# Retention's v projected with tokens as rows, in a hybrid decoder layer

## The reference

```python
proj = hn @ w_in
..., rq, rk, rv, rg, gate_a, gate_b = jnp.split(proj, SPLIT_IDX, axis=-1)
rq = rotary(rq.reshape(B, L, RET_HEADS, RET_DK), pos)
rk = rotary(rk.reshape(B, L, RET_HEADS, RET_DK), pos)
o_b = retention_chunked(rq, rk, rv.reshape(B, L, RET_HEADS, RET_DV))
...
inner = einsum('bhncs,bhnse->bhnce', einsum('bhncd,bhnsd->bhncs', q, k) * dmask, v)
def step(S, xs):
    in_c, qd_c, kd_c, v_c = xs
    o_c = in_c + jnp.einsum('bhcd,bhde->bhce', qd_c, S)
    S = S * g_chunk + jnp.einsum('bhcd,bhce->bhde', kd_c, v_c)
    return S, o_c
```

## Time and profile before

| | |
|---|---|
| median of 3 runs | 2141.28 us (2135.45 to 2142.12) |
| the profiled execution: its time | 2140.7 us |
| the profiled execution: its span | 2138.9 us |
| TensorE busy | 2085.0 us (97%) |
| VectorE busy | 1134.9 us (53%) |
| ScalarE busy | 634.3 us (30%) |
| GpSimd busy | 287.6 us (13%) |
| mean granted TensorE clock | 0.991 of full speed |
| line 733, projection matmuls | 5688 in three groups of 1896, 618.2 + 610.6 + 608.5 us busy |
| share of the last chain on TensorE | 85% |

### The profile page before, as it was taken

The page is one execution under the profiler, slowest core; times in us unless marked ns, Lnnn a source line. Parts: engine busy times, 40 slices in busy tenths (PEclk is TensorE's granted clock), DMA queues, the critical chain, the costliest instruction groups (busy, mean ns, idle before and its releaser), DMA issues.

```text
span 2138.9 us, 30674 instructions
## 1 busy us (share of the span) xinstructions
PE 2085.0 (97%) x13250; PEld 2003.1 (94%) x13250; DVE 1134.9 (53%) x1283; ACT 634.3 (30%) x805; POOL 287.6 (13%) x277
## 2 busy tenths in 40 slices
PE   7999999989999999999999999999999999999997
PEld 6999999989999999999999999999999999999995
DVE  4443454766656655556534333365656455565556
ACT  4212323533333443353433332321111111111112
POOL 0000002586360212112100001100000000000002
PEclk9999999989999999999999999999999999999999
DMA  7222225654444554454342321120111111111102
GB/s 207 80 107 93 81 93 175 217 168 111 128 128 128 154 158 136 120 131 125 98 155 91 116 79 50 40 89 30 50 50 59 41 39 50 50 50 32 58 30 79
DMA packets 156764, 207.36 MB, mean 97 GB/s; under 512 B 33230, under 2 KB 118102, under 8 KB 156502
## 3 DMA queue, kind: packets, MB, share of 16 engines
q1 hardware_dynamic: 156630, 205.40, 30.8%
HBM read 151.85 MB, written 53.52 MB: 96 GB/s over the span
## 4 chain that ended last, share of the span: by engine, by line
PE 85%; DVE 5%; POOL 3%; DMA 2%; ACT 2%; issue 2%; SPq 0%; POOLq 0%; DVEq 0%; ACTq 0%
PE a_psum L733 33%; PE a_psum L138 29%; PE a_psum L1012 11%; PE a_psum L801 1%; PE a_psum L718 1%; DVE post L1400 1%; POOL ext L1789 1%; PE a_psum L818 1%; POOL y L1785 1%; PE a_psum L798 1%; PE a_psum L741 1%; PE a_psum L844 1%; PE a_psum L921 1%; DMA w_raw<-in_w_in 1%; PE a_psum L936 1%
## 5 line engine op out<-in xcount | busy, mean ns | idle before, releaser
L733 PE MATMUL a_psum<-xh,w_hi 128*128 128x348 f32 (+1 forms) x1896 | 618.2, 326 | 4.8 <-ACT post L1126 3.7
L733 PE MATMUL a_psum<-xl,w_hi 128*128 128x348 f32 (+1 forms) x1896 | 610.6, 322 | 0.0
L733 PE MATMUL a_psum<-xh,w_lo 128*128 128x348 f32 (+1 forms) x1896 | 608.5, 321 | 0.0
L733 PEld LDWEIGHTS a_psum<-xh,w_hi 128*128 128x128 f32 x1896 | 358.6, 189 | 9.2 <-ACT post L1126 4.6
L733 PEld LDWEIGHTS a_psum<-xl,w_hi 128*128 128x128 f32 x1896 | 358.9, 189 | 0.7
L733 PEld LDWEIGHTS a_psum<-xh,w_lo 128*128 128x128 f32 x1896 | 358.5, 189 | 0.0
L1126 ACT ACTIVATE post<-a_psum 128x348 f32<-128x348 f32 (+1 forms) x234 | 107.2, 459 | 611.6 <-PE a_psum L733 585.6
L1058 ACT ACTIVATE w_hi<-w_raw 128x1024 fp32r<-128x1024 f32 x131 | 138.3, 1055 | 436.8 <-PE a_psum L138 409.3
L138 PE MATMUL a_psum<-xh,w_hi 128*128 128x342 f32 (+1 forms) x1104 | 234.4, 320 | 6.2 <-DVE xl L1352 6.2
L138 PE MATMUL a_psum<-xl,w_hi 128*128 128x342 f32 (+1 forms) x1104 | 234.5, 320 | 0.0
L1333 DVE TENSOR_TENSOR w_lo<-w_raw,w_hi 128x1024 fp32r<-128x1024 f32 x131 | 168.4, 1286 | 123.4 <-ACT w_hi L1058 123.4
(11 more groups left out here) (209 smaller groups left out, 2546.6 us busy)
## 6 DMA issues: line engine op xcount, KB each, us to landing
w_raw<-in_w_in SPq DMA_DIRECT2D x79, 512.0 KB, 3.6
mix_scratch<-post SPq DMA_DIRECT2D x48, 522.0 KB, 3.1
w_raw<-in_w_up SPq DMA_DIRECT2D x44, 512.0 KB, 3.5
ext<-mix_scratch SPq DMA_DIRECT2D x9, 1536.0 KB, 8.5
y<-mix_scratch SPq DMA_DIRECT2D x27, 512.0 KB, 5.6
down_raw<-in_w_ffn_down SPq DMA_DIRECT2D x22, 512.0 KB, 4.5
ext<-grow_scratch SPq DMA_DIRECT2D x9, 512.0 KB, 5.5
ext<-mix_scratch SPq DMA_DIRECT2D x9, 512.0 KB, 6.8
```

What stands on the lines that cost most here:

```text
L733: mm = pe.matmul(psum[:, u % 2, 0:n], w[:, k, :], x[:, k, at0 + n * j:at0 + n * j + n], start=(k == 0 and part == 0), stop=(k == KC - 1 an ...
```

## The change

Tokens become the rows of v's projection: the stationary operand is a block of x (128 channels by the tokens of a chunk, 16 for the first), the moving one is 512 or 256 columns of weights. The 24 units of v are now 9 of one chunk with 512 columns (the first four weight tiles), then 7 and 8 units with 256 columns, of one or two chunks each (`RV_STEPS`). The four tiles of the first part are all split before its first unit, into `va` in the memory of `y`; the next two go to the usual slots and the last two to `vb2` in `y`. `front_plan` gets its own places for these loads and splits. Each unit is stored by itself into a new DRAM scratch `rvt` (chunk, token, channel) from two stage buffers, and `r_load` loads a chunk of it as it is used, in two buffers (`rvs`). `r_trv` and its copy are gone; `r_in` has 16 tiles rather than 24. Since `y` is taken until the first part is done, `inv` waits for it (`RV_B`), its first batch begins behind u = 34 (before: 38), with `tout` 0 and `tin` 1 behind u = 55 and `comp` 8 behind u = 59, and the `mst` steps stand behind u = 28, 29, 31, 32, 34, 37, 40, 43, 46 (before: 29, 31, 34, 36, 39, 41, 44, 46, 49). The core of the diff:

```diff
+RV_STEPS = ([(0, 512, (c,)) for c in range(9)]
+            + [(512, 256, c) for c in ((0,), (1,), (2, 3), (4, 5), (6,), (7,), (8,))]
+            + [(768, 256, c) for c in ((0,), (1,), (2,), (3, 4), (5,), (6,), (7,), (8,))])
+RV_A, RV_B, RV_C = 3 * T_RV, 3 * T_RV + 9, 3 * T_RV + 16
...
+    splits_at = {(T_RV - 2, 1): (T_RV,), (T_RV - 2, 2): (T_RV + 1,), (T_RV - 1, 0): (T_RV + 2,), (T_RV - 1, 1): (T_RV + 3,),
+                 (T_RV, 0): (T_RV + 4,), (T_RV, 2): (T_RV + 5,), (T_RV + 3, 0): (T_RV + 6,), (T_RV + 3, 2): (T_RV + 7,)}
+    loads_at = {(T_RV - 3, 1): (T_RV,), (T_RV - 3, 2): (T_RV + 1,), (T_RV - 2, 1): (T_RV + 2, T_RV + 3),
+                (T_RV - 1, 1): (T_RV + 4,), (T_RV, 0): (T_RV + 5,), (T_RV, 2): (T_RV + 6,), (T_RV + 3, 0): (T_RV + 7,),
+                (T_RV + 3, 2): (T_Q,)}
...
-        at = 29 + 5 * c // 2
+        at = (28, 29, 31, 32, 34, 37, 40, 43, 46)[c]
...
-    u = 38
+    u = 34
     for b in range(NBATCH):
         steps[u].append(("tin", b))
         if b == 1:
-            steps[u].append(("comp", NCH - 1))
+            steps[u + 4].append(("comp", NCH - 1))
...
-        u += 1
+        u += 5 if b == 0 else 1
         steps[u].append(("tout", b))
...
+                    if T_RV <= t < T_Q:
+                        pe.wait_ge(w_lo, T_RV + (4 if u < RV_B else 6 if u < RV_C else 8))
+                        pe.wait_ge(evac, u - 1)
+                        at0, n, chunks = RV_STEPS[u - RV_A]
+                        for i, c in enumerate(chunks):
+                            rows_ = META if c == 0 else CH
+                            x0 = FRONT if c == 0 else FRONT + META + CH * (c - 1)
+                            for k in range(KC):
+                                hi, lo = ((x[:, k, :] for x in va) if u < RV_B else (x[:, :, k, :] for x in vb1)
+                                          if u < RV_C else (x[:, k, :] for x in vb2))
+                                for part, (w, x) in enumerate(((hi, xh), (hi, xl), (lo, xh))):
+                                    mm = pe.matmul(psum[0:rows_, u % 2, n * i:n * i + n], x[:, k, x0:x0 + rows_], w,
+                                                   start=(k == 0 and part == 0), stop=(k == KC - 1 and part == 2))
+                        mm.then_inc(units_done, 1)
+                        continue
...
-                elif kind == "r_trv":
-                    c = a[0]
-                    if c + 1 < NCH:
-                        pe.wait_ge(d_rkd, c + 1)
-                    else:
-                        pe.wait_ge(d_rS, 4 * c)
-                    turn(r_in[:, 16:24, :], 2).then_inc(pe_rtv, 1)
                 elif kind == "r_out":
                     c = a[0]
-                    pe.wait_ge(a_rv, c + 1)
+                    pe.wait_ge(rv_ld[c % 2], 16 * (c // 2 + 1))
...
-                    sp.dma_start(r_in, mix[:, S_RQ:S_RQ + 24, c * CH:c * CH + CH]).then_inc(r_ld, 16)
+                    sp.dma_start(r_in, mix[:, S_RQ:S_RQ + 16, c * CH:c * CH + CH]).then_inc(r_ld, 16)
+                    if c == 0:
+                        for n in range(2):
+                            sp.wait_ge(rv_stored[n], 16 * 12)
+                        sp.wait_ge(units_done, 3 * T_Q)
+                    elif c >= 2:
+                        sp.wait_ge(pe_rst, 4 * (c - 1))
+                        sp.wait_ge(pe_ro, c - 1)
+                    sp.dma_start(rvs[c % 2].rearrange("p h c -> p (h c)"), sc["rvt"][c]).then_inc(rv_ld[c % 2], 16)
...
                     if j0 == 0:
+                        pool.wait_ge(units_done, RV_B)
                         pool.wait_ge(d_tout, 2 * b)
```

More of the change, by code:

```diff
@@ L165, in front_plan @@
     add = plan.append
+    splits_at = {(T_RV - 2, 1): (T_RV,), (T_RV - 2, 2): (T_RV + 1,), (T_RV - 1, 0): (T_RV + 2,), (T_RV - 1, 1): (T_RV + 3,),
[3 more added lines that the diff above has]
+                (T_RV + 3, 2): (T_Q,)}
     def unit(t, j):
-        if j == 0:
+        if j == 0 and not T_RV - 1 <= t < T_Q - 1:
             add(("split", t + 1))
+        for n in splits_at.get((t, j), ()):
+            add(("split", n))
         add(("proj", t, j))
     def weights(t, j):
-        if j == 0:
+        if j == 0 and not T_RV - 2 <= t < T_Q - 1:
             add(("load", t + 2))
+        for n in loads_at.get((t, j), ()):
+            add(("load", n))
     add(("intro",))
@@ L240, in front_plan @@
         weights(t, j)
-        if j == 2:
-            add(("conv", t) if conv_tile(t) else ("rvstore", t))
+        if not conv_tile(t):
+            add(("rvstore", 3 * t + j))
+        elif j == 2:
+            add(("conv", t))
     units = [(t, j) for t in range(T_ZB, T_END) for j in range(3)]
@@ L355, in program @@
         w_raw = sb("w_raw", [P, KC, P])
-        wh = [sb(f"w_hi{s}", [P, KC, P], F32R) for s in range(SLOTS)]
-        wl = [sb(f"w_lo{s}", [P, KC, P], F32R) for s in range(SLOTS)]
+        wh2, wl2 = (sb(n, [P, SLOTS, KC, P], F32R) for n in ("w_hi", "w_lo"))
+        wh, wl = ([x[:, s, :, :] for s in range(SLOTS)] for x in (wh2, wl2))
         post = [sb(f"post{s}", [P, T]) for s in range(5)]
@@ L371, in program @@
         o_hi, o_lo = sb("o_hi", [P, GH, P], F32R), sb("o_lo", [P, GH, P], F32R)
+        row_bytes = 4 * T
+        va = [sb(f"v_w4_{n}", [P, KC, 4 * P], F32R, over=place["y"] + 4 * row_bytes * n) for n in range(2)]
+        vb1 = [wh2, wl2]
+        vb2 = [sb(f"v_w2b_{n}", [P, KC, 2 * P], F32R, over=place["y"] + 2 * row_bytes * n) for n in range(2)]
+        diag = sb("diag", [P, GH, P], over=place["o_hi"])
+        rv_st = sb("rv_stage", [P, 2, 512], over=place["o_lo"])
         free = place["a_cst"] + -(-4 * C_HEAD // 32) * 32
@@ L410, in program @@
         abT = y[0:2 * GH, 0:2, :].rearrange("p k t -> p (k t)")[:, 0:TW]
-        rkd, rv, rqd, r_osq, r_ro, r_ost = (yrow(n) for n in range(6))
-        xtmp, diag = y[:, 6, 0:256], yrow(7)
-        r_in = erow(0, 3072)
+        rkd, rqd, r_osq, r_ro, r_ost = (yrow(n) for n in (0, 2, 3, 4, 5))
+        rvs = (yrow(1), erow(2048))
+        xtmp = y[:, 6, 0:256]
+        r_in = erow(0, 2048)
         rS = ext[:, 3072:5120].rearrange("p (h a e) -> p h a e", h=RH, a=2)
@@ L539, in stored_up_to @@
                 for n in range(2):
-                    sp.wait_ge(stored[n], 16 * (8 + sum(1 for m in range(T_K, t + 1) if m % 2 == n)))
+                    sp.wait_ge(stored[n], 16 * (8 + sum(1 for m in (*range(T_K, T_RV), *range(T_Q, T_ZB))
+                                                        if m <= t and m % 2 == n)))
             for step in plan:
@@ L797, in _ @@
                             o = four(4 + n // 4)[:, n % 4, seen(c)]
-                            mm = pe.matmul(o, rv[:, n, :], rsc[:, h, seen(c)], start=True, stop=(c == 0))
+                            mm = pe.matmul(o, rvs[c % 2][:, n, :], rsc[:, h, seen(c)], start=True, stop=(c == 0))
                             if c:
@@ L1107, in _ @@
                     elif T_RV <= t < T_Q:
[L1108 to L1110 removed]
+                        if u >= RV_A + 2:
+                            act.wait_ge(rv_stored[u % 2], 16 * ((u - RV_A) // 2))
+                        n, rows_ = RV_STEPS[u - RV_A][1] * len(RV_STEPS[u - RV_A][2]), CH
+                        if RV_STEPS[u - RV_A][2] == (0,):
+                            rows_ = META
+                        dst, src = rv_st[0:rows_, u % 2, 0:n], psum[0:rows_, u % 2, 0:n]
                     elif t < T_ZB:
```

75 lines of the change are left out of this document (49 added, 26 removed).

## The result

| | before | after |
|---|---|---|
| median, run beside each other | 2138.84 us (2135.45 to 2142.12) | 2124.51 us of six runs, 2124.18 us of the five that the ratio uses |
| ratio after / before | | 0.9932 (95% interval 0.992 to 0.9944) |
| the profiled execution: its time | 2140.7 us | 2124.18 us |
| its span | 2138.9 us | 2122.4 us |
| mean granted TensorE clock | 0.991 | 0.995 |

The changed kernel takes 0.68% less by the ratio (14.5 us), 14.7 us less by the median of its five runs, and 16.5 us less by the two profiled executions; the forecast had 15.7 us between profiled executions, and 2125.0 us. Five of the six runs of the changed kernel lie between 2121.88 and 2127.12 us; the sixth took 4149 us and has no part in the ratio.

What follows compares the result with a forecast made beforehand. TensorE, busy 97% of the span, and its few waits bound the kernel. +9.4 - 8.3 - 13.0 - 5.8 + 2.0 = -15.7 us against 2140.7 us gave 2125.0 us (chance 0.69), range 2115 to 2141 us.

Steps and rivals of the forecast that it cites:

- Term 1: v's projection as rows: 216 matmuls of 512 columns and 432 of 256 (0.117 us, unmeasured) replace 576: +9.4 us.
- Rival C: Matmuls of 256 columns don't run at the longer ones' rate; at 0.231 us each +49.1 us, 2174 us; chance 0.08.
- Term 2: Nine groups of eight transpositions of v go from TensorE, 0.92 us each: -8.3 us.
- Term 3: TensorE's 8.6 us wait before line 798 (`r_out` 0) and 4.4 us of low clock behind it go: -13.0 us.
- the edit takes this chain apart twice: Before line 798: no copy of v left to wait for, and `comp` 8 moves behind `tin` 1; within the -13.0 us.
- The layout of the inversion: GpSimd's inversion begins at 393.5 us and ends near 458, `tout` 0 is due near 472; no longer last.
- Rival D: The wait moves: the inversion holds `r_out` or the next loads, Term 3 gives half; 2132 us; chance 0.06.
- Term 4: TensorE's waits for `rkd` (line 1441) in two chunks, 4.2 us, and 1.6 us of lower clock go: -5.8 us.
- Term 5: Work moved and added around v's projection and Retention's first state copies: +2 us, between 0 and 12.
- (b, c): In v's stage, short units' evacuations (margins 1.5 and 0.7 us) and SP's 24 stores: 1 us together.
- rival B: Between steps 37 and 47 short units outrun ScalarE, VectorE and stores: 12 us instead of 2, 2135 us; chance 0.17.
- (e): At step 55 `tout` 0 and `tin` 1 stand before Retention's first state copies on VectorE: 1 us.

## Why the prediction was right

**Term 1 (+9.4): right.** v's projection takes 101.1 us for 101 predicted. 512 columns came every 0.232 us (0.2335), 256 every 0.118 (0.117). The unmeasured price was the step by which the forecast could most easily fall, and it lay on the line through the two rows. Rival C is out. The 7.7 to 8.3 us of the meta tokens' leftover products confirm that columns set the cost, however few are stationary.

**Term 2 (-8.3): right.** Eight groups added again cost 7.2 to 8.7 us, 7.4 in the stage; nine at that price are 8.3.

**Term 3 (-13.0): the size was right, the reason half wrong.** The wait and the low clock are both gone (26.64 us busy at 1.00 in the 27 us where it was 18.41 at 0.75). But "the edit takes this chain apart twice" failed: each cut was counted as enough by itself. Moving `comp` 8 alone is enough (13.0 us over the stretch of the wait, 12.7 in the median). Taking away the copy of v alone isn't: with `comp` 8 beside `tin` 1 the changed kernel loses 7.0 us in the stage, since line 1241 is held. The prediction asked who needs the copy of v, not what stands next in ScalarE's order behind the held copies. The layout of the inversion held; GpSimd in the changed kernel:

```profile
397.08 0.95 POOL L1852 MEMSET ext<- 128x1024 f32 x1
...
453.75 1.27 POOL L1864 TENSOR_TENSOR ext<-ext,y 128x31 f32<-128x31 f32 x1
```

It began 3.6 us later than the 393.5 predicted and ended at 455.0, 3 us earlier than 458; `tout` 0 was at 471.2 (472). Rival D is out for the changed kernel; in the kernel with exchanged turns and the old places of the inversion it was there, 4.19 us.

**Term 4 (-5.8): right in kind, the size not shown.** Put back, the wait costs 7.3 us in the stage and 8.9 in the median, but this is the wait of the new plan (5.7 us); in the old plan it was 4.2 us of waiting and 1.6 of clock. The 1.6 was one execution's: with `comp` 8 moved alone, the clock stayed at 1.00 behind the same wait.

**Term 5 (+2): right in size, from one of its parts.** The feeding (b, c) cost 0 and not 1: the stage of v has no wait. The evacuation that step 41 needs was laid out for 411.6, that for step 47 at 435.6; ScalarE's rows:

```profile
408.71 2.71 ACT L1264 ACTIVATE ext<-post 32x256 f32<-32x256 f32 x4 [3.31 <-DVE post L1566]
...
411.45 0.87 ACT L1206 ACTIVATE rv_stage<-a_psum 128x256 f32<-128x256 f32 x2
...
431.04 2.76 ACT L1264 ACTIVATE ext<-post 32x256 f32<-32x256 f32 x4 [2.22 <-DVE post L1566]
...
434.78 0.64 ACT L1206 ACTIVATE rv_stage<-a_psum 128x256 f32<-128x256 f32 x2
```

Each row of line 1206 holds two evacuations, and the unit needs the first of the two. That one ended at 411.83, 0.34 us ahead of the start of the unit's first matmul at 412.17 (predicted margin 1.5), and at 435.14, 0.49 ahead of the one at 435.63 (predicted margin 0.7). Margins of a few tenths, and double copies do break them (2.9 us): rival B didn't happen, but it was near. The state copies (e) cost 0.36 us at step 55, where I had 1, and the same kind of wait for line 1543 cost 1.4 + 0.8 us at other chunks, 2.6 us in all and 1.8 more than before. The prediction had no such waits at other chunks, so that the 2 us came out is partly luck.

```profile
479.56 1.97 PE L889 MATMUL a_psum<-y 128*128 128x256 f32 x8 [0.36 <-DVE ext L1541]
...
508.17 1.97 PE L889 MATMUL a_psum<-ext,y 128*128 128x256 f32 x8 [1.16 <-DVE ext L1543]
```

**The sum.** In the stage (-16.1), +9.5 for the projection and -8.3 for the turns leave -17.3 us for the waits, the clock and what is added; the prediction had -13.0 - 5.8 + 2.0 = -16.8. What the prediction didn't ask is what the same plan would do without v as rows: 2122.64 us, no slower than the change.

## What to carry to other kernels

An instruction that waits on an in-order engine holds all that stands behind it; to cost the removal of one thing held, write down what is next in the queue and who needs that, since it inherits the wait. Here one line that moved four small copies later was worth 13 us, and the larger rewrite beside it gave nothing that exchanging two steps didn't give too. When a change has a rewrite and a new order in it, run the new order alone; and swapping two steps may lose a wait as well as deleting one of them.

## What the runs showed of the hardware beyond that

- The moving operand's layout made no difference: `vb1` (two slots a tile apart; all of the piece at 386.14) and `vb2` (one run of 256 columns; all of the piece at 412.41) both came every 0.118 us (14.21 / 120 and 11.37 / 96).
- The lower clock came behind some waits and not behind others of the same length. With `comp` 8 early on the changed kernel, line 889 took 3.45 us behind its 5.82 us wait (granted clock 0.60 over 3.8 us), against 1.97 behind one of 0.36; with exchanged turns, line 815 took 3.75 us behind 4.19 (0.50). Behind 1.16 us it still took 1.97. In between it went either way. Behind 2.72 us the clock fell in the kernel before and behind 2.71 us it stayed at 1.00 with `comp` 8 alone; behind 2.25 us it fell in that same run (0.50 from 486.5 to 488.5 us) and behind 2.27 us it stayed at 1.00 with `comp` doubled.
- How long it stays low differs too. Behind the same wait near 1110 us (3.14 and 3.17 us) the changed kernel had 0.50 for 3 us in one profile and for 6 us in the other, which cost the second 1.5 us more. Differences of 1 or 2 us between two single profiles can come from this alone.
